# The outputs of an attention pair issued straight behind the next scores, in both attentions of the second block

## The reference

```python
def sliding_window_branch(q, k, v, z, sinks, cos, sin):      # 16 query heads of 64, 4 key heads
    q, k = rope(q), rope(k)
    # blocks of 128 queries against their own and the block before, 256 keys
    scores = jnp.einsum('bnqkgd,bnskd->bnkgqs', qb, kb).astype(jnp.float32) * (HEAD_DIM ** -0.5)
    scores = jnp.where(mask, scores, -jnp.inf)
    probs = jax.nn.softmax(jnp.concatenate([scores, sink], axis=-1), axis=-1)[..., :-1]
    out = jnp.einsum('bnkgqs,bnskd->bnqkgd', probs.astype(v.dtype), vb)
    return out.reshape(b, s, SWA_HEADS * HEAD_DIM) * jax.nn.silu(z)

def forgetting_attention_branch(q, k, v, f_logit, z, f_bias):  # 16 heads of 64, causal
    cum = jnp.cumsum(log_sigmoid(f_logit + f_bias))
    for i in range(s // FOX_BLOCK):                            # 4 blocks of 128 queries
        sc = jnp.einsum('bqhd,bkhd->bhqk', q[:, start:end], k[:, :end]) * scale
        sc = sc + cum[:, :, start:end, None] - cum[:, :, None, :end]
        probs = jax.nn.softmax(jnp.where(causal, sc, -jnp.inf), axis=-1)
        outs.append(jnp.einsum('bhqk,bkhd->bqhd', probs, v[:, :end]))
    return concatenate(outs) * jax.nn.silu(z)
```

## Time and profile before

| what | us |
|---|---|
| median of 3 runs | 3656.58 |
| the 3 runs | 3652.99 to 3659.28 |
| the profiled execution | 3653.08 |
| its span, first to last instruction | 3651.2 |
| PE busy | 3457.1 (95% of the span) |
| POOL busy | 2124.1 (58%) |
| DVE busy | 1536.8 (42%) |
| ACT busy | 816.6 (22%) |

### The profile page before, as it was taken

How to read it: one execution, slowest core, us unless ns; L and a number is a source line. 1 busy time by engine, 2 the same in 40 slices (tenths; PEclk the granted TensorE clock), 3 DMA queues, 4 the chain that set the end, 5 groups by cost and what they waited for, 6 DMA issues and landing times.

```text
span 3651.2 us, 49401 instructions
## 1 busy us (share of the span) xinstructions
PE 3457.1 (95%) x17270; PEld 2764.3 (76%) x17270; DVE 1536.8 (42%) x2814; ACT 816.6 (22%) x1659; POOL 2124.1 (58%) x2116
## 2 busy tenths in 40 slices
PE   7999889999999899998999999999989999999998
PEld 6777778887777678886887678777868777777776
DVE  4555431104555431106673652332367636523323
ACT  1133111101123111002221540333022225403320
POOL 5745456766745457665556556444746565564455
PEclk9999999999999999998999999999999999999999
DMA  3211122222211122222122222111212121121111
GB/s 127 81 58 69 63 76 103 92 95 79 81 58 69 69 81 92 101 95 92 59 80 81 70 73 90 70 59 70 94 70 81 58 92 70 70 93 68 60 70 69
DMA packets 39930, 285.38 MB, mean 78 GB/s; under 512 B 4688, under 2 KB 5200, under 8 KB 5728
## 3 DMA queue, kind: packets, MB, share of 16 engines
q1 hardware_dynamic: 38880, 282.13, 21.4%
q10 hardware_dynamic: 896, 1.14, 0.1%
HBM read 281.15 MB, written 2.10 MB: 78 GB/s over the span
## 4 chain that ended last, share of the span: by engine, by line
PE 80%; DVE 11%; issue 4%; ACT 3%; POOL 1%; DMA 0%; DVEq 0%; ACTq 0%; POOLq 0%
PE banks L358 20%; PE banks L360 19%; PE banks L359 19%; PE banks L597 2%; PE banks L595 2%; PE banks L596 2%; PE banks L910 1%; PE banks L934 1%; PE banks L921 1%; PE banks L566 1%; PE banks L913 1%; PE banks L719 1%; ACT rot_q L1224 1%; DVE rtmp L1367 1%; PE banks L955 1%
## 5 line engine op out<-in xcount | busy, mean ns | idle before, releaser
L321 POOL TENSOR_SCALAR whi<-raw 128x512 fp32r<-128x512 f32 x1056 | 731.6, 702 | 1490.8 <-PE banks L360 1240.8
L326 POOL TENSOR_TENSOR wlo<-raw,whi 128x512 fp32r<-128x512 f32 x1056 | 1437.2, 1371 | 0.0
L358 PE MATMUL banks<-xhi,whi 128*128 128x512 f32 x2976 | 1220.2, 410 | 40.9 <-DVE xlo L1387 15.0
L360 PE MATMUL banks<-xhi,wlo 128*128 128x512 f32 x2976 | 1169.5, 393 | 0.0
L359 PE MATMUL banks<-xlo,whi 128*128 128x512 f32 x2976 | 1167.4, 392 | 0.0
L358 PEld LDWEIGHTS banks<-xhi,whi 128*128 128x128 f32 x2976 | 564.1, 190 | 189.8 <-issue 33.4
L360 PEld LDWEIGHTS banks<-xhi,wlo 128*128 128x128 f32 x2976 | 562.8, 189 | 124.1
L359 PEld LDWEIGHTS banks<-xlo,whi 128*128 128x128 f32 x2976 | 564.7, 190 | 109.4 <-issue 6.7
L358 PE MATMUL banks<-yhi,whi 128*128 128x512 f32 x544 | 216.9, 399 | 17.0 <-DVE ylo L1557 5.6
L359 PE MATMUL banks<-ylo,whi 128*128 128x512 f32 x544 | 213.1, 392 | 0.0
L360 PE MATMUL banks<-yhi,wlo 128*128 128x512 f32 x544 | 213.0, 392 | 0.0
(11 more groups left out here) (259 smaller groups left out, 4324.6 us busy)
## 6 DMA issues: line engine op xcount, KB each, us to landing
raw<-weights SPq DMA_DIRECT2D x264, 1024.0 KB, 4.8
x<-x_in SPq DMA_DIRECT2D x1, 2048.0 KB, 8.3
out<-merged SPq DMA_DIRECT2D x1, 2048.0 KB, 6.3
rot<-const SPq DMA_DIRECT2D x1, 512.0 KB, 11.7
rot<-const ACTq DMA_DIRECT2D x1, 512.0 KB, 3.3
wide_mask<-const ACTq DMA_DIRECT2D x1, 384.0 KB, 4.0
wide_mask<-const SPq DMA_DIRECT2D x1, 256.0 KB, 12.5
cst<-const SPq DMA_DIRECT2D x1, 232.0 KB, 8.4
```

The lines of the kernel that those rows point to most:

```text
L321: pool.tensor_scalar(whi[p][:, w], raw[p][:, w], 1.0, 1.0, ALU.mult, ALU.mult).then_inc(s("hi_written"), 1)
L326: return pool.tensor_tensor(wlo[p][:, w], raw[p][:, w], whi[p][:, w].bitcast(F32), ALU.subtract)
L358: pe.matmul(dst, whi[p][:, w], hi[:, k, :], start=start and i == 0, stop=False)
L360: mm = pe.matmul(dst, wlo[p][:, w], hi[:, k, :], start=False, stop=stop and last_k)
```

## The change

In both loops the outputs of pair k-1 are issued straight behind the scores of pair k+1, ahead of the step's fill and of both turns. Before they stood between the fill and the second turn. Nothing else is changed: no instruction is added or removed, and the queues of DVE, ACT, POOL and SP are the same row for row.

```diff
                     if k + 1 < SWA_STEPS:
                         swa_scores(k + 1)
+                    if k:
+                        swa_output(k - 1)
                     if k == 0:
                         parts = 5
                     else:
...
                     else:
                         swa_turn(2 * k)
                         fill(parts, 3 * len(products) // 4)
-                    if k:
-                        swa_output(k - 1)
                     swa_turn(2 * k + 1)
                     fill(3 * len(products) // 4, len(products))
...
                     if k + 1 < STEPS:
                         fox_scores(k + 1)
+                    if k:
+                        fox_output(k - 1)
                     fill(0 if k else 3, 4)
                     fox_turn(2 * k)
                     fill(4, 6)
-                    if k:
-                        fox_output(k - 1)
                     fox_turn(2 * k + 1)
                     fill(6, 8)
```

## The result

| | before | after |
|---|---|---|
| median, us | 3655.05 | 3677.54 |
| runs, us | 3652.99 to 3659.28 (4) | 3676.92 to 3681.06 (4) |
| the profiled execution's span, us | 3651.2 | 3676.1 |
| sliding-window attention, first to last scores (L804), us, layer 1 / 2 | 174.0 / 173.6 | 181.7 / 182.4 |
| forgetting attention, first to last scores (L910), us, layer 1 / 2 | 247.0 / 247.0 | 250.0 / 250.0 |

The change makes the kernel slower: the ratio of after to before is 1.0062 with a 95% interval of 1.0045 to 1.0079, +22.5 us. I had said +12.8 and 3667, with a range that ended at 3677. The direction was right and the size was not. Between their first and last scores the two attentions account for +16.5 and +5.8 us, together 22.3.

A forecast was written before the change was run, and what follows sets the result against it. PE, busy 95% of the span, was taken to bound the kernel. Terms 3.1 - 3 + 2.6 + 6.0 + 0.8 + 3.3 = +12.8 us gave 3665.9 on the profiled execution, forecast as 3667, range 3655 to 3677.

The forecast's parts named there:

- neighbours, forgetting attention: Forgetting attention: outputs following gate matmuls on the array cost 0.05 us more for each of 62 moved pairs, +3.1 us.
- second turns, forgetting attention: Forgetting attention: second turns of 16 pairs with three transposes wait 0.16 us for ACT's copy, +2.6 us; with four, none.
- neighbours, sliding-window: Sliding-window attention: outputs straight behind the half-height scores save 0.17 us, 30 times, -5 us at most; taken as -3.
- four waits for `swa_read`: Sliding-window steps 4 and 8, two layers: a group's first outputs wait for DVE's gating, some 2.4 us each.
- what is given back around them, and the second group's scores: Sliding-window attention: 1.1 us returned per place, net wait cost +1.5 each; pair 4's scores wait 0.8 us longer a layer.
- halved clock: Behind PE waits of about 2 us or more: two of six bring the 1.2 GHz level, +3.3 us, ends 0 and +9.9.
- counting changes alone: Both attentions: pricing only tiling mode changes gives 0 and -3 us for the neighbours together, 3 less than the forecast's terms.
- the rotary work on DVE follows ... so the copies start at 2062.0 and `swa_read` comes at about 2071.3: Sliding-window step 4: gating ends 9.0 to 9.4 us behind the copies' start, now later, so PE waits some 2.4 us.
- the 16 outputs of pair 5 are already done, 1.1 us given back: Sliding-window attention, behind step 5's later waits: pair 5's outputs no longer follow there, returning 1.1 us; net +1.5 a place.
- The gating was not in time: Rival, sliding-window attention: DVE's gating precedes the scores' end, 6.0 becomes -3, total +1.3, about 3654 to 3658; chance 0.22.
- The faster rival: Rival, both attentions: outputs ride free behind scores, 92 pairs save about 0.12 us each, gating in time, about 3642; chance 0.04.
- all second turns: Rival, forgetting attention: second turns of two, three and four transposes wait, 11 us instead of 2.6, about 3675; chance 0.07.

The follow-up runs named there:

- last experiment on it: Forgetting-attention part of the change alone, with three fill products instead of two between the turns, against the kernel before: 3655.11 us, ratio 1.0001 (0.9992 to 1.0010).

## Why the prediction was right and wrong

Each term, against what the traces and runs gave. The measured neighbour terms come from distances of starts, in the forgetting attention as what is left of 5.8 without the waits, in the sliding-window one over two steps without a wait (from the scores at 2154.96 to those at 2172.03 in before, 17.07 us, and from 2161.57 to 2178.34 in after, 16.77; the next such two 17.07 and 16.79), 0.14 us a pair. The sliding-window terms count what lies between the first and the last scores.

| term | forecast | measured | from |
|---|---|---|---|
| neighbours, forgetting attention | +3.1 | +2.5 to +2.8 | last experiment on it; distances |
| second turns, forgetting attention | +2.6 | +3.0 to +3.4 | distances, 1.5 a layer; last experiment on it, 1.7 |
| neighbours, sliding-window | -3 | -4.2 | 30 x 0.14 |
| four waits for `swa_read` | 9.6 (4 x 2.4) | 14.5 | waits |
| what is given back around them, and the second group's scores | -2.8 | -0.2 | what is left of 16.5 |
| halved clock | +3.3 | +6.4 | 4 x 1.6 |

**The forgetting attention** was right: 5.7 forecast, 5.8 measured, and for the two reasons named. That the sum is this close is partly luck, since one term came out lower and the other higher. The waits are 0.14 or 0.17 us with three transposes; the neighbour price is 0.04 us a pair where I had 0.05. The one wait with four transposes, 0.24 us a layer, I had excluded. The Trainium skill (TensorEngine Tiling (Array Packing), Key Properties) names a drain at each mode change without a price; counting changes alone gave 0 here, and the runs gave 2.5 to 2.8 us. In the sliding-window attention the count gave -3 and the pairs -4.2. The distances between starts were nearer in the first and no worse in the second.

**The sliding-window attention** was wrong in size: 7.1 forecast, 16.5 measured. Three steps failed.

The step "the rotary work on DVE follows ... so the copies start at 2062.0 and `swa_read` comes at about 2071.3" moved DVE's work as a rigid block. From ACT's first copy the rotary work started as before (+4.43 us, +4.41 in before), but POOL's L321 at +4.36 instead of +4.53, so that it was now ahead of DVE's first operation and not behind it, and the three rotary operations took 4.35 us instead of 3.36. (That the copies start at 2061.69 where I had 2062.0 is partly luck: this execution's attention begins 1.5 us earlier.) Rows 11 to 14 did not show POOL; I had priced "0.5 us more on DVE" only as an end. With PE 0.4 us earlier than I had worked out, the wait became 3.6.

The step "Not every gap of that size need be followed by one. I take two of six" failed: all four gaps of 3.6 us were followed by a halving, and the two of 1.7 us by none. Part of this may hang on the step before: the gaps became longer than the 2.4 us that I had priced.

The step "the 16 outputs of pair 5 are already done, 1.1 us given back" failed: a third of that was given back. From the scores of pair 7 to those of pair 8 before took 16.31 us (2083.76 to 2100.07) and after takes 15.81 (2087.52 to 2103.33), and 0.14 of the difference is the neighbours'. The wait for DVE (L1863) ahead of which the outputs now stand is 1.3 us in both kernels: the chain that it waits for came later too. Over the four places that is some 3 us less than I had credited, about what the entry is off. The other waits between first and last scores, added up over both layers, change by -0.6 us: the scores of pair 4 (0.5 a layer), the turns behind DVE (0.5 a layer) and the outputs of pair 5 and 9 for ACT's copy (0.14 each) wait longer, and the waits for POOL (2.3) and for the value copies (0.9) are gone. That leaves 0.4 us without an explanation; I did not follow it up. A term is only given back where no chain on ACT or DVE is next in line, and the experiment that kept pairs 4 and 8 in place showed that chain bare, at 2.2 us.

One wait was nowhere in my sum. In the last step there are no scores ahead of the outputs of pair 14, and they wait for ACT's copy, once a layer:

```profile
2195.86 0.88 PE L831 MATMUL banks<-work,v 128*64 128x128 f32 x12 [0.62 <-ACT work L1191]
```

This lies behind the last scores (2187.40) and so adds 0.6 us a layer to what the stretches show.

**The rivals.** The gating was not in time. The faster rival, outputs that ride free behind the scores, failed on the neighbours: they gain 0.14 us a pair in one attention and lose 0.04 in the other. In the forgetting attention the first output starts 0.20 to 0.33 us behind the last gate matmul, where in before the fill (but for two waits) started 0.11 to 0.23 behind it: the 0.10 us of the way in, as priced, and not the free ride that a distance below 0.2 would have shown. Second turns with one or two transposes did not wait, so "all second turns" was wrong too. The range was too narrow: with the 0.5 us I granted DVE and six halvings the sum reached 3676, and the runs needed 1.2 us on the wait, four halvings and next to nothing given back.

## What to carry to other kernels

When a step is moved up in an in-order queue, two things move against each other: the work ahead of which it now stands starts later, and the engine itself comes sooner to the next wait. Work out both arrivals from one common event, with the other engines' work laid beside it again, and ask which chain is next in line before anything is credited as given back. Where an early consumer waits behind work that it does not need, reordering the producer's queue is the cheap cure: swapping two steps in DVE's queue turned the sliding-window part's +16 us into -4.

## What the hardware showed

**DVE and POOL block each other for whole operations.** A rotary operation of DVE with two operands in SBUF (L1825, 128x512) takes 0.69 us alone. In before it starts ahead of POOL's L321 (2065.41 against 2065.53): it takes 0.71, and POOL's operation 1.06 instead of 0.62. In after POOL is first (2066.05), and DVE takes 1.08. Caught behind a whole L326 a DVE operation takes 1.64 to 1.82 us, and L326, 1.29 alone, then takes about 1.7. The Trainium skill (SBUF — State Buffer, Who interferes with whom) says that a DVE instruction with two SBUF inputs contends with a GpSimd instruction that reads SBUF, and that the one that issues first blocks the other. The traces agree with both: neither engine is slowed in proportion, and the durations fit each waiting for the end of the other's operation. POOL's L321 going from 0.12 us behind the chain's first operation to 0.07 ahead of it therefore made the chain 1.0 us longer.

**What followed a gap of PE.** In the sliding-window attentions, over the profiles of all kernels of this study, PE's gap of 3.6 us ahead of the outputs was followed by the 1.2 GHz level 12 times in 12, that of 2.2 us in the kernel that kept pairs 4 and 8 in place 4 times in 4, the gap of 2.0 ahead of a second turn 25 times in 26, and the one of 1.6 to 1.7 ahead of the scores of pair 4 once in 16. The clock fell between 1.6 us before and 1.3 us after PE's restart. I had expected far less to hang on some tenths of a microsecond. Each such halving cost 1.1 to 1.6 us on top of the gap.

The length of the gap alone does not decide it, though. Elsewhere in the same traces, with the clock at 1.00 before them, PE's gaps of 2.2 to 2.8 us ahead of L358 and L477 were followed by the lower level only 19 times in 73, and the gap of 3.7 to 3.8 us ahead of L412 25 times in 26. The same gap, in work that both kernels share, in before and in after:

```profile
1683.68 0.49 PE L358 MATMUL banks<-xhi,whi 128*128 128x512 f32 x1 [2.30 <-POOL wlo L326]
1685.00:1688.30 3.30, 3.30 (x9) 2.53 (x8) 0.07 (x1) 3.12 (x3) 3.30 (x5) 0.50 0.74 295
```

```profile
1681.95 0.49 PE L358 MATMUL banks<-xhi,whi 128*128 128x512 f32 x1 [2.29 <-POOL wlo L326]
1683.00:1686.40 3.40, 3.40 (x17) 2.80 (x16) 0.00 (x0) 3.37 (x3) 3.40 (x5) 1.00 0.77 296
```

So a gap of 3.6 us is to be priced with its halving. One of 2 to 3 us may bring it or not, and what decides between them no run here shows.
